# Hyena branch of a two-layer encoder: half-length transforms by even and odd samples, short convolution read from PSUM, and the branch's steps set between projection units

## Chip, cores and metric

The kernel runs on one core of one Trainium2 chip. The metric is the device time of one execution of the whole program, two encoder layers, in microseconds (us). The names of the engines in the profile are PE (TensorE, matrix products), PEld (its weight loads), DVE (VectorE), ACT (ScalarE), POOL (GpSimd) and SP (SyncE, which issues the weight loads from memory).

## What is computed

Two layers over 512 positions of width 1024: a gated feed-forward block, a mixer with three branches, cross-attention to a memory of 256 positions, and a second feed-forward block. The change touches the middle branch of the mixer, the bidirectional Hyena branch of 256 channels:

```python
uc = short_conv(p, conv_w, conv_b)      # three taps over time, per channel
v, x1, x0 = jnp.split(uc, 3, axis=-1)
h = hyena_filters(...)                  # three sine layers of width 64, then w4, times exp(-t * |decay|)
z = x1 * v
# bidir_long_conv: filter = [h_fwd, 0, reversed h_bwd], length 2L
y = irfft(rfft(z, 2L) * rfft(filter), 2L)[:L] + skip * z
return x0 * y
```

The other two branches are a neighbourhood attention ("A") and a dilated attention ("C"), six heads each. All three read the same normed input through one projection.

## The kernel before

**Units.** All large products run as units. A unit is a 128 x 1024 slice of weights: SP loads it into one of two `raw` tiles, ScalarE rounds it to a high half (`high`, L256), VectorE subtracts to get the low half (`low`, L261), and PE multiplies high and low halves of weights and input in 48 instructions of 256 columns (`unit`, L322 to L326). Four units of halves can be ready ahead (`RING`). The result lies in a PSUM bank until an engine has read it out and counted up the semaphore `evac`.

**The mixer's part.** Six Hyena units come first, U_HY = 66 to 71, called Hyena units 0 to 5 here. The first four of them go through `first_units` (L376 to L378) in two halves, since the normed input arrives in halves; 4 and 5 follow as ordinary units. ScalarE copies each result with its neighbours' borders into `p` (L822), VectorE makes the short convolution from it with one instruction of scale and bias and two that add a neighbour (L1101, L1105). Then come 18 units for values, queries and keys of the two attentions, U_VA = 72 to 89, called V0 to V17 here. VectorE copies each out, and V0 to V5 (the values) are then turned by PE in `turn_values`. After V15 attention begins.

**The order of the work** is written out by hand: each engine has a list, and the engines wait for each other at semaphores only. In the list of PE all Hyena steps stand between Hyena unit 4 and V0. They are: three small products for the sine layers (L546, L552), each of which waits for the sine of the one before (L830), which waits for five VectorE steps that reduce the argument (L1117 to L1125); the taps (L556); eight transposes of z (L563); the transforms of the filter (L574) and of z (L583), each 2 parts x 4 blocks of frequency x 4 blocks of time with 256 columns; the product of the spectra on VectorE (L1151 to L1159); the way back (L592), 16 products of 512 columns; and the sums of squares for the norm (L597). Every F32 product shows as two records in the trace. The transforms are products with tables of cosine and sine, `fwd` and `inv`, 2 MB each, which GpSimd's queue loads in every layer.

**GpSimd** also loads the bias strips of attention A (48 small transfers, L1300) once the Hyena branch has left its buffers, and then makes 18 subtractions (L1306) of them before attention may start; the buffers of the Hyena branch and of attention lie in the same memory (`place`), so their order is held by semaphores (`wait_apart`).

Of the kernel before, what the change touches and what calls it, by code (L numbers as in the profile page):

```python
# [36 lines left out]
STRIP = 7 * P  # L37

# [27 lines left out]
def build(nc, x, mem, par, grow, w_first, w_second, w_proj, rpb, t5, fw1, fw23, fw4, fvec, decay,  # L66
          k_emb, k_fwd, k_inv, k_time, k_namask, k_hot, k_lnn, k_eye, out):
    with ExitStack() as ctx:
# [34 lines left out]
        def place(parts):  # L103
# [11 lines left out]
        hH, hL = hid["hH"], hid["hL"]  # L115
        hy = place([
            ("p", [P, 6, T + 2], F32), ("uc", [P, 6, T], F32), ("fwd", [P, 2, 4, T], F32),
            ("inv", [P, 2, 4, T], F32), ("filt", [P, 2, 4, 256], F32), ("taps", [P, 4, 512], F32),
            ("even", [P, 4, 256], F32), ("zt", [P, 4, 256], F32), ("emb", [P, T], F32),
            ("w1", [P, FW], F32), ("w2", [P, FW], F32), ("w3", [P, FW], F32), ("w4", [P, 512], F32),  # L120
            ("fv", [P, 8], F32), ("tneg", [P, 4], F32)])
        at = place([
            ("qA", [P, 3, T], F32), ("kA", [P, 3, T], F32), ("vt", [P, 3, T], F32),
            ("VA", [P, 7, 384], F32), ("biasA", [P, 3, NA_H, 256], F32), ("qC", [P, 3, T], F32),
            ("kC", [P, 3, T], F32), ("VC", [P, 4, 384], F32), ("strip", [P, C_H, STRIP], F32)])


        ac = place([
            ("over_qA", [P, 3, T], F32), ("over_kA", [P, 3, T], F32), ("kCh", [P, 3, T], F32R),
            ("over_VA", [P, 7, 384], F32), ("qCh", [P, 3, T], F32R), ("over_biases", [P, 2, NA_H, 256], F32),  # L130
            ("qCl", [P, 3, T], F32R), ("kCl", [P, 3, T], F32R)])
# [8 lines left out]
        rstrip = strip[:].rearrange("p h n -> p (h n)")[:, 0:NA_H * 384].rearrange(  # L140
            "p (h r c) -> p h r c", h=NA_H, r=WR)
        amask = strip[:].rearrange("p h n -> p (h n)")[:, NA_H * 384:NA_H * 384 + 768].rearrange(
            "p (y n) -> p y n", y=3)
# [36 lines left out]
        pad_zero = sem("pad_zero")  # L180
# [12 lines left out]
        filt_ready = sem("filt_ready")  # L193
        zt_mm = sem("zt_mm")
        zt_ready = sem("zt_ready")
        z_mm = sem("z_mm")
        prod = sem("prod")
        y_mm = sem("y_mm")
# [118 lines left out]
        def _(e):  # L317
# [221 lines left out]
            for L in range(LAYERS):  # L539
# [4 lines left out]
                first_units(u0, 4 * L + 1)  # L544
                e.wait_ge(hy_small, L * 112 + 112)
                e.matmul(bank[4][0:FW, :], hy["w1"][0:EMB, :], hy["emb"][0:EMB, :], start=True,  # L546
                         stop=True).then_inc(f_mm, 1)
                for j in (4, 5):
                    e.wait_ge(evac, E0 + j - 3)
                    unit(u0 + j, u_of, ul_of, j % 4)  # L550
                    e.wait_ge(f_sin, L * 3 + j - 3)
                    e.matmul(bank[4][0:FW, :], hy[f"w{j - 2}"][0:FW, :], tmp[3][0:FW, :], start=True,  # L552
                             stop=True).then_inc(f_mm, 1)
                e.wait_ge(f_sin, L * 3 + 3)
                for m in range(4):
                    e.matmul(bank[4 + m][:], tmp[3][0:FW, m * P:m * P + P], hy["w4"][0:FW, :],  # L556
                             start=True, stop=True).then_inc(taps_mm, 1)
                for half in range(2):
                    e.wait_ge(z_ready, L * 2 + 2)
                    e.wait_ge(taps_ready, L * 7 + half + 1)  # L560
                    for tt in (2 * half, 2 * half + 1):
                        for c in range(HYT):
                            mm = e.transpose(bank[4 + half][:, (tt % 2 * 2 + c) * P:(tt % 2 * 2 + c) * P + P],  # L563
                                             hy["uc"][:, c, tt * P:tt * P + P], eye[:])
                    mm.then_inc(zt_mm, 1)
                e.wait_ge(taps_ready, L * 7 + 7)
                e.wait_ge(hy_loaded, L * 48 + 48)
                e.wait_ge(zt_ready, L * 2 + 2)
                for part in range(2):
                    for half in range(2):  # L570
                        for kt in (2 * half, 2 * half + 1):
                            for m in range(4):
                                rhs = hy["even"][:, m, :] if part == 0 else hy["taps"][:, m, 256:512]
                                mm = e.matmul(bank[4 + 2 * part + half][:, kt % 2 * 256:kt % 2 * 256 + 256],  # L574
                                              hy["fwd"][:, part, m, kt * P:kt * P + P], rhs,
                                              start=m == 0, stop=m == 3)
                        mm.then_inc(filt_mm, 1)
                e.wait_ge(filt_ready, L * 4 + 4)
                for part in range(2):
                    for half in range(2):  # L580
                        for kt in (2 * half, 2 * half + 1):
                            for m in range(4):
# [888 lines left out]
```

## Time and profile before

| | us |
|---|---|
| median of three runs | 2685.17 (2684.04 to 2689.0) |
| the profiled execution, its own time | 2689.14 |
| its span in the trace | 2687.3 |
| PE busy | 2585.8 (96%) |
| VectorE busy | 1027.3 (38%) |
| ScalarE busy | 923.3 (34%) |
| GpSimd busy | 112.9 (4%) |
| mean granted clock of TensorE | 0.98 |

The busy time of an engine is the time in which at least one of its instructions runs. Products overlap in PE's pipeline, so the time that one more product costs is the distance between starts, and not the duration printed with one. The granted clock is a share of 2.4 GHz; 0.5 is the lower level, 1.2 GHz. "Idle before" names the engine and line whose end released the waiting one.

### The profile page before, as it was taken

To read this page: it belongs to the slowest core of one execution; us is meant where nothing else is said; L and a number is where in the kernel's file an instruction comes from. 1 tells how busy PE (TensorE), PEld (TensorE's weight loads), DVE (VectorE), ACT (ScalarE), POOL (GpSimd) and SP (SyncE) were. 2 spreads that over 40 slices of the span, in tenths; PEclk is the share of its full clock that TensorE was granted. 3 is DMA by queue.
4 is the path that set the end of the run, shared out by engine and by line. 5 is a ranking of instruction groups with operands and counts; after the bars stand their busy time and mean duration, and the time that the engine had idled before them with its cause. 6 is when DMAs were issued, how large, how long until landed. Compare 5 with 4: busy or idle time off the path is not lost.

```text
span 2687.3 us, 47605 instructions
## 1 busy us (share of the span) xinstructions
PE 2585.8 (96%) x20484; PEld 2470.9 (92%) x20484; DVE 1027.3 (38%) x1351; ACT 923.3 (34%) x1509; POOL 112.9 (4%) x186
## 2 busy tenths in 40 slices
PE   7999997899999899999999999978999999999998
PEld 7999996698799799999999999966978998999998
DVE  3333236234445453332253332443443643533322
ACT  4333233024533343332253331331254433533322
POOL 0000000140000000000000000103200000000000
PEclk9999997999999999999999999979999999999999
DMA  4322324041024122333232322321300341233222
GB/s 147 94 93 94 99 75 156 22 138 48 1 94 139 52 96 94 94 95 98 87 111 94 94 94 95 117 95 48 136 25 25 102 142 40 95 94 94 94 95 79
DMA packets 66247, 240.62 MB, mean 90 GB/s; under 512 B 8882, under 2 KB 10632, under 8 KB 65088
## 3 DMA queue, kind: packets, MB, share of 16 engines
q1 hardware_dynamic: 57600, 209.74, 24.0%
q0 software_dynamic: 8368, 28.83, 3.3%
q8 instruction: 107, 1.75, 0.3%
q14 instruction: 28, 0.23, 0.0%
q10 hardware_dynamic: 144, 0.07, 0.0%
HBM read 236.48 MB, written 2.12 MB: 89 GB/s over the span
## 4 chain that ended last, share of the span: by engine, by line
PE 88%; DVE 6%; DMA 3%; ACT 2%; issue 1%; POOL 0%; DVEq 0%; ACTq 0%; POOLq 0%
PE bank L322 23%; PE bank L326 23%; PE bank L324 23%; PE bank L515 3%; DMA raw<-in_w_proj 2%; PE bank L490 2%; PE bank L376 2%; PE bank L378 2%; PE bank L377 2%; DVE wl L261 2%; PE bank L574 1%; PE bank L592 1%; PE bank L457 1%; PE bank L583 1%; PE bank L464 1%
## 5 line engine op out<-in xcount | busy, mean ns | idle before, releaser
L261 DVE TENSOR_TENSOR wl<-raw,wh 128x1024 fp32r<-128x1024 f32 x392 | 486.4, 1241 | 482.0 <-ACT wh L256 480.7
L322 PE MATMUL bank<-uH,wh 128*128 128x256 f32 x3328 | 664.4, 281 | 0.0
L326 PE MATMUL bank<-uH,wl 128*128 128x256 f32 x3328 | 661.1, 280 | 0.0
L324 PE MATMUL bank<-uL,wh 128*128 128x256 f32 x3328 | 660.9, 280 | 0.0
L256 ACT ACTIVATE wh<-raw 128x1024 fp32r<-128x1024 f32 x392 | 413.3, 1054 | 706.8 <-PE bank L326 586.1
L322 PEld LDWEIGHTS bank<-uH,wh 128*128 128x128 f32 x3328 | 507.5, 189 | 7.2 <-issue 7.1
L324 PEld LDWEIGHTS bank<-uL,wh 128*128 128x128 f32 x3328 | 507.2, 188 | 0.0
L326 PEld LDWEIGHTS bank<-uH,wl 128*128 128x128 f32 x3328 | 507.0, 188 | 0.0
L973 DVE TENSOR_TENSOR tmp<-bank,tmp 128x512 f32<-128x512 f32 x88 | 60.8, 691 | 629.5 <-PE bank L326 596.8
L322 PE MATMUL bank<-wh,hH 128*128 128x256 f32 x1408 | 281.6, 281 | 0.0
L326 PE MATMUL bank<-wh,hL 128*128 128x256 f32 x1408 | 281.1, 281 | 0.0
L324 PE MATMUL bank<-wl,hH 128*128 128x256 f32 x1408 | 281.1, 281 | 0.0
L326 PEld LDWEIGHTS bank<-wh,hL 128*128 128x128 f32 x1408 | 215.9, 188 | 0.0
L324 PEld LDWEIGHTS bank<-wl,hH 128*128 128x128 f32 x1408 | 215.9, 188 | 0.0
L322 PEld LDWEIGHTS bank<-wh,hH 128*128 128x128 f32 x1408 | 215.7, 188 | 0.0
L734 ACT ACTIVATE hH<-tmp 128x512 f32 x88 | 55.9, 636 | 404.1 <-DVE tmp L973 404.1
L376 PE MATMUL bank<-uH,wh 128*128 128x256 f32 x512 | 146.5, 286 | 9.9 <-DVE uL L940 4.9
L377 PE MATMUL bank<-uL,wh 128*128 128x256 f32 x512 | 144.1, 281 | 0.0
L378 PE MATMUL bank<-uH,wl 128*128 128x256 f32 x512 | 143.9, 281 | 0.0
L731 ACT ACTIVATE tmp<-bank 128x512 f32<-128x512 f32 x88 | 52.5, 597 | 204.9 <-PE bank L326 190.5
L322 PE MATMUL bank<-wh,uH 128*128 128x256 f32 x512 | 105.7, 289 | 6.9 <-DVE uL L1050 3.9
L376 PEld LDWEIGHTS bank<-uH,wh 128*128 128x128 f32 x512 | 97.3, 190 | 11.7 <-DVE wl L261 6.3
(198 smaller groups left out, 2959.0 us busy)
## 6 DMA issues: line engine op xcount, KB each, us to landing
raw<-in_w_first SPq DMA_DIRECT2D x176, 512.0 KB, 3.6
raw<-in_w_proj SPq DMA_DIRECT2D x128, 512.0 KB, 3.5
raw<-in_w_second SPq DMA_DIRECT2D x88, 512.0 KB, 3.5
strip<-bias_of_distance POOLq DMA_DIRECT2D x2, 2688.0 KB, 13.3
g_pre<-in_grow POOLq DMA_DIRECT2D x8, 512.0 KB, 7.2
g_post<-in_grow POOLq DMA_DIRECT2D x8, 512.0 KB, 4.9
fwd<-in_k_fwd POOLq DMA_DIRECT2D x4, 1024.0 KB, 7.0
inv<-in_k_inv POOLq DMA_DIRECT2D x2, 2048.0 KB, 9.4
```

The source lines that it names most:

```text
L256: e.activation(wh[u % RING][:], raw[u % RAWS][:], ACT.Copy).then_inc(high_ready, 1)
L261: e.tensor_tensor(wl[u % RING][:], raw[u % RAWS][:], wh[u % RING][:].bitcast(F32), ALU.subtract).then_inc(split_ready, 1)
L322: e.matmul(b[:, c], still_h, hi[:, c], start=first and c.start == 0, stop=False)
L324: e.matmul(b[:, c], still_h, lo[:, c], start=False, stop=False)
L326: mm = e.matmul(b[:, c], still_l, hi[:, c], start=False, stop=last and c.stop == n)
L376: e.matmul(bank[j][:, n], wh[u % RING][:, w], uH[:, k, n], start=half + k == 0, stop=False)
L377: e.matmul(bank[j][:, n], wh[u % RING][:, w], uL[:, k, n], start=False, stop=False)
L378: mm = e.matmul(bank[j][:, n], wl[u % RING][:, w], uH[:, k, n], start=False, stop=half == 1 and k == DT - 1)
L490: mm = e.transpose(bank[2 + t % 2][:, c * P:c * P + P], tmp[t % 4][:, c * P:c * P + P], eye[:])
L515: mm = e.matmul(O[:, col:col + w], tmp[4 + t % 2][:, c * P:c * P + P], v, start=c == 0, stop=c == chunks - 1)
L734: e.activation(hH[:, bass.ds((2 * it + q) * T, T)], tmp[2 + q][:], ACT.Copy).then_inc(hidh_ready, 1)
L973: e.tensor_tensor(tmp[2 + q][:], bank[2 * q + 1][:], tmp[q][:], ALU.mult).then_inc(h_ready, 1)
```

## The change

**Transforms.** The frequencies run in pairs: the table now holds the lower half of them only (256), and the samples are sorted by parity (`by_parity`). The spectrum of the even samples and that of the odd samples are made apart, each with half the samples and half the frequencies, and their sum and difference give the two halves of the spectrum (`butterflies`). The way back does the same in reverse: four sums and differences on VectorE, then an even and an odd half of y with 256 columns each. The tables are half as large, and z is taken with stride 2 when it is transposed.

**Short convolution.** ScalarE reads a unit's bank with the middle tap as scale and the bias added and writes `uc` (`middle`); VectorE adds the two neighbours with the bank itself as input (`neighbours`). `p` and its borders are gone, and VectorE's second step counts up `evac`.

**Order.** The small products of the sine layers stand behind the first and third Hyena unit and behind unit 4; z is transposed between Hyena units 4 and 5. The spectrum of z stands before V0, and the rest between the V units: taps behind V0, spectrum of the filter behind V1, the way back behind V4, the sums behind V6, with VectorE's steps in its own list at the same places. Since these steps hold banks 4 to 7, `turn_values` uses banks 2 and 3, and V0 to V5 alternate between banks 0 and 1.

**GpSimd.** `inv` is loaded ahead of a wait that it stood behind; the bias strips wait for the transforms of z, the taps and the windows instead of for the finished branch, and their subtractions for the way back.

The diff, cut to its core:

```diff
-            def first_units(u0, b):
+            def first_units(u0, b, between=lambda j: None):
...
                             mm.then_inc(unit_done, 1)
+                            between(j)
...
+                def spectrum(part, parity, moving):
+                    for kt in range(2):
+                        for m in range(2):
+                            mm = e.matmul(bank[4 + 2 * part + parity][:, kt * 256:kt * 256 + 256],
+                                          hy["fwd"][:, part, parity, m, kt * P:kt * P + P], moving[:, 2 * parity + m, :],
+                                          start=m == 0, stop=m == 1)
+                    return mm
+
+                first_units(u0, 4 * L + 1, lambda j: filter_layer(j // 2) if j in (0, 2) else None)
+                e.wait_ge(evac, E0 + 1)
+                unit(u0 + 4, u_of, ul_of, 0)
+                filter_layer(2)
+                e.wait_ge(z_ready, L * 2 + 2)
...
+                e.wait_ge(evac, E0 + 2)
+                unit(u0 + 5, u_of, ul_of, 1)
+                e.wait_ge(hy_loaded, L * 48 + 48)
+                e.wait_ge(zt_ready, L * 2 + 2)
+                e.wait_ge(f_arg, L * 3 + 3)
                 for part in range(2):
...
+                    for parity in range(2):
+                        mm = spectrum(part, parity, hy["zt"])
+                    mm.then_inc(z_mm, 1)
...
+                        for parity in range(2):
+                            for part in range(2):
+                                for kt in range(2):
+                                    cut = slice(kt * 256 + c * P, kt * 256 + c * P + P)
+                                    mm = e.matmul(bank[4 + c][:, parity * 256:parity * 256 + 256],
+                                                  yc[:, 2 * part + parity, cut], hy["inv"][:, part, parity, kt, :],
+                                                  start=part + kt == 0, stop=part + kt == 2)
...
+                hyena = {0: filter_taps, 1: filter_spectrum, 4: back_to_time, 6: hyena_sums}
...
                 for j in range(18):
-                    e.wait_ge(evac, E0 + 6 + j - 3)
-                    unit(L * UNITS + U_VA + j, u_of, ul_of, (6 + j) % 4)
+                    e.wait_ge(evac, E0 + 6 + j - (1 if j < 8 else 3))
+                    if j == 8:
+                        e.wait_ge(vt_out, L * 9 + 9)
+                    unit(L * UNITS + U_VA + j, u_of, ul_of, j % 2 if j < 6 else (6 + j) % 4)
+                    if j in hyena:
+                        hyena[j]()
...
+                    e.activation(hy["uc"][:, UC[j], :], bank[j % 4][:], ACT.Identity,
+                                 scale=pr[:, CW0 + 6 + j:CW0 + 6 + j + 1],
+                                 bias=pr[:, CB0 + j:CB0 + j + 1]).then_inc(conv_mid, 1)
                     high(e, u + RING)
...
+                middle(0)
+                argument(0)
+                middle(1)
+                sine(0)
+                middle(2)
+                argument(1)
+                middle(3)
+                sine(1)
+                middle(4)
+                argument(2)
...
+                    e.wait_ge(conv_mid, L * 6 + j + 1)
+                    e.scalar_tensor_tensor(c[:, 1:T], b[:, 0:T - 1], before, c[:, 1:T], ALU.mult,
+                                           ALU.add).then_inc(conv, 1)
+                    e.wait_ge(conv, L * 6 + j + 1)
+                    e.scalar_tensor_tensor(c[:, 0:T - 1], b[:, 1:T], after, c[:, 0:T - 1], ALU.mult,
+                                           ALU.add).then_inc(evac, 1)
...
+                        if part == 0:
+                            e.tensor_tensor(to[:, 1, :], even, odd, ALU.subtract).then_inc(ready, 1)
+                        else:
+                            e.tensor_tensor(to[:, 3, :], odd, even, ALU.subtract).then_inc(ready, 1)
...
+                for j in range(4):
+                    neighbours(j)
+                    low(e, u0 + j)
+                    if j in (0, 2):
+                        reduced(j // 2)
...
+                butterflies(hy["zf"], zf_even, zf_ready)
+                hyena = {0: tap_values, 1: real_product, 2: imaginary_product, 4: gated, 6: hyena_norm}
...
                     low(e, L * UNITS + U_VA + j + RING)
+                    if j in hyena:
+                        hyena[j]()
...
+                e.dma_start(hy["inv"][:], k_inv).then_inc(inv_loaded, 16)
                 wait_apart(e, u_ready, (4 * L + 1) * NT + NT)
                 e.dma_start(tmp[0][:], decay[L:L + 1].to_broadcast([P, 512])).then_inc(hy_loaded, 16)
-                e.dma_start(hy["inv"][:], k_inv).then_inc(inv_loaded, 16)
                 gains(L, 4 * L + 2)
 
-                wait_apart(e, hyout, L * 6 + 4)
+                wait_apart(e, z_mm, L * 2 + 2)
+                wait_apart(e, taps_mm, L * 4 + 4)
+                wait_apart(e, window, L * 4 + 4)
...
+                wait_apart(e, y_mm, L * 2 + 2)
                 for y, c0 in enumerate((16, 8, 0)):
```

How the lists move, at three places. First PE's list before, layer 0, from Hyena unit 4 to V0 (the rows `bank<-uH,wh` are the first product of a unit; `tmp,w` are the sine layers, `w,tmp` the taps, `eye,uc` the transposes of z, the last row with `tmp,ones` the sums):

```order
L322 MATMUL bank<-uH,wh 128x256 [waits split_ready,evac]
...
L552 MATMUL bank<-tmp,w 64x512 [waits f_sin]
L556 MATMUL bank<-w,tmp 128x512 [waits f_sin]
...
L563 MATMUL bank<-eye,uc 128x128 [waits taps_ready,z_ready]
...
L574 MATMUL bank<-even,fwd 128x256 [waits zt_ready,hy_loaded,taps_ready]
...
L574 MATMUL bank<-taps,fwd 128x256 x16
L583 MATMUL bank<-zt,fwd 128x256 [waits filt_ready]
L583 MATMUL bank<-zt,fwd 128x256 x31
L592 MATMUL bank<-inv,taps 128x512 [waits inv_loaded,prod]
L592 MATMUL bank<-inv,taps 128x512 x15
L597 MATMUL bank<-tmp,ones 128x512 [waits hysq] x2
L322 MATMUL bank<-uH,wh 128x256 [waits split_ready,evac]
```

All of it lies in a row, from the second sine layer to the sums, without a unit in between. Now PE's list after the change, from Hyena unit 4 to the spectrum of the filter behind V1:

```order
L328 MATMUL bank<-uH,wh 128x256 [waits split_ready,evac]
...
L560 MATMUL bank<-tmp,w 64x512 [waits f_sin]
L580 MATMUL bank<-eye,uc 128x128 [waits z_ready]
...
L328 MATMUL bank<-uH,wh 128x256 [waits split_ready,evac]
...
L566 MATMUL bank<-zt,fwd 128x256 [waits f_arg,zt_ready,hy_loaded]
L566 MATMUL bank<-zt,fwd 128x256 x15
L328 MATMUL bank<-uH,wh 128x256 [waits split_ready,evac]
...
L598 MATMUL bank<-w,tmp 128x512 [waits zf_ready,f_sin]
...
L328 MATMUL bank<-uH,wh 128x256 [waits split_ready,evac]
...
L566 MATMUL bank<-even,fwd 128x256 [waits taps_ready]
L566 MATMUL bank<-even,fwd 128x256 x7
L566 MATMUL bank<-taps,fwd 128x256 x8
```

Between each two Hyena steps stands a unit, the product of z with `fwd` has moved ahead of the taps, and it and that of the filter have half their instructions. Last VectorE's list after the change, from the copy of V1 (`vt<-bank`) on, where `wl` is a weight's low half, `zf` and `filt` are the spectra, and `Y` their product:

```order
L1296 COPY vt<-bank 128x8x64 [waits unit_done]
L267 TENSOR_TENSOR wl<-raw,wh 128x1024 [waits high_ready]
L1198 TENSOR_TENSOR filt<-filt,bank 128x512 [waits filt_even]
L1200 TENSOR_TENSOR filt<-bank,filt 128x512 [waits filt_even]
L1204 TENSOR_TENSOR filt<-filt,bank 128x512 [waits filt_ready] x2
L1232 TENSOR_TENSOR Y<-zf,filt 128x1024 [waits filt_ready,zf_ready]
L1233 TENSOR_TENSOR even<-zf,filt 128x1024
L1235 TENSOR_TENSOR Y<-Y,even 128x1024 [waits prod]
L1296 COPY vt<-bank 128x8x64 [waits unit_done]
L267 TENSOR_TENSOR wl<-raw,wh 128x1024 [waits high_ready]
L1239 TENSOR_TENSOR Y<-zf,filt 128x1024
L1241 TENSOR_TENSOR even<-zf,filt 128x1024 [waits prod]
```

Behind the copy of V1 the filter's butterflies and the real product now stand, and the copy of V2 comes behind them; before, no Hyena step stood behind any of these copies.

## Rows read from the trace of the kernel before

**Rows 1.** The page: span, busy time of the engines, chain that ended last.
```profile
span 2687.3 us, 47605 instructions
...
PE 2585.8 (96%) x20484; PEld 2470.9 (92%) x20484; DVE 1027.3 (38%) x1351; ACT 923.3 (34%) x1509; POOL 112.9 (4%) x186
...
PE 88%; DVE 6%; DMA 3%; ACT 2%; issue 1%; POOL 0%; DVEq 0%; ACTq 0%; POOLq 0%
```

**Rows 2.** Windows of layers 0 and 1; the columns are in the first line.
```profile
core 0: us, PE busy (x) PEld busy (x) DVE busy (x) ACT busy (x) POOL busy (x), PEclk, DMA share, GB/s
426.30:525.70 99.40, 75.28 (x284) 51.73 (x284) 36.26 (x54) 20.27 (x28) 1.17 (x3) 0.81 0.09 33
525.70:625.00 99.30, 99.30 (x849) 98.84 (x848) 36.64 (x36) 22.95 (x29) 43.40 (x66) 1.00 0.40 129
1755.30:1854.60 99.30, 75.04 (x293) 51.70 (x292) 36.34 (x55) 21.02 (x30) 2.08 (x4) 0.83 0.11 36
1854.60:1954.00 99.40, 99.40 (x847) 98.47 (x846) 41.61 (x37) 22.64 (x29) 41.53 (x65) 1.00 0.39 127
```

**Rows 3.** PE's waits, 426.3 to 525.7: line, releaser, total us, times, longest.
```profile
PE bank L592 <- DVE taps L1159: 8.0, 1, 8.0
PE bank L556 <- ACT tmp L830: 6.3, 1, 6.3
PE bank L552 <- ACT tmp L830: 6.0, 1, 6.0
...
PE bank L583 <- ACT filt L847: 0.7, 1, 0.7
```

**Rows 4.** PE's timeline, 426 to 530: start, us, line, tiles, count, idle before.
```profile
439.12 1.96 PE L552 MATMUL bank<-tmp,w 64*64 64x512 f32 x2 [6.00 <-ACT tmp L830]
...
448.77 1.07 PE L552 MATMUL bank<-tmp,w 64*64 64x512 f32 x2
...
456.15 7.19 PE L556 MATMUL bank<-w,tmp 64*128 64x512 f32 x8 [6.31 <-ACT tmp L830]
463.27 1.97 PE L563 MATMUL bank<-eye,uc 128*128 128x128 f32 x8
...
484.53 14.08 PE L583 MATMUL bank<-zt,fwd 128*128 128x256 f32 x64 [0.69 <-ACT filt L847]
506.56 15.79 PE L592 MATMUL bank<-inv,taps 128*128 128x512 f32 x32 [7.95 <-DVE taps L1159]
522.19 1.02 PE L597 MATMUL bank<-tmp,ones 128*128 128x512 f32 x2
```

**Rows 5.** VectorE's timeline, 395 to 585.
```profile
419.18 1.54 DVE L1105 SCALAR_TENSOR_TENSOR uc<-p,pr,uc 128x512 f32<-128x512 f32 x2
420.64 1.22 DVE L261 TENSOR_TENSOR wl<-raw,wh 128x1024 fp32r<-128x1024 f32 x1
...
435.65 0.41 DVE L1117 TENSOR_SCALAR tmp<-tmp 64x512 f32<-64x512 f32 x1
...
458.82 0.69 DVE L1130 TENSOR_TENSOR taps<-bank,tmp 128x512 f32<-128x512 f32 x1 [3.39 <-ACT tmp L839]
...
531.42 1.22 DVE L1180 COPY vt<-bank 128x512 f32<-128x512 f32 x1 [2.81 <-PE bank L326]
...
557.35 2.02 DVE L261 TENSOR_TENSOR wl<-raw,wh 128x1024 fp32r<-128x1024 f32 x1 [0.46 <-ACT wh L256]
```

**Rows 6.** ScalarE's timeline, 395 to 585.
```profile
428.92 1.06 ACT L256 ACTIVATE wh<-raw 128x1024 fp32r<-128x1024 f32 x1 [4.75 <-DMA raw<-in_w_proj]
...
431.31 0.76 ACT L827 ACTIVATE tmp<-bank,fv 64x512 f32<-64x512 f32 x1
432.09 1.28 ACT L830 ACT_TABLE_LOAD   x1
438.44 0.63 ACT L830 ACTIVATE tmp<-tmp 64x512 f32<-64x512 f32 x1 [5.06 <-DVE tmp L1125]
```

**Rows 7.** GpSimd's timeline, 395 to 760.
```profile
525.07 25.02 POOL L1300 DMA_DIRECT2D strip<-in_rpb  x48
551.90 18.14 POOL L1306 TENSOR_TENSOR biasA<-strip 128x256 f32<-128x256 f32 x18 [1.80 <-DMA strip<-in_rpb]
```

More of the change, by code:

```diff
@@ L197, in build @@
         prod = sem("prod")
+        y_ready = sem("y_ready")
         y_mm = sem("y_mm")
@@ L543, in _ @@
                 u0 = L * UNITS + U_HY
[L544 to L553, printed above, removed]
@@ L578, in _ @@
[L578 to L582, printed above, removed]
-                                mm = e.matmul(bank[6 - 2 * part + half][:, kt % 2 * 256:kt % 2 * 256 + 256],
-                                              hy["fwd"][:, part, m, kt * P:kt * P + P], hy["zt"][:, m, :],
-                                              start=m == 0, stop=m == 3)
-                        mm.then_inc(z_mm, 1)
@@ new lines, in filter_spectrum, with back_to_time @@
+                def filter_spectrum():
+                    e.wait_ge(taps_ready, L * 7 + 7)
+                    for part in range(2):
+                        for parity in range(2):
+                            mm = spectrum(part, parity, hy["even"] if part == 0 else hy["taps"][:, :, 256:512])
+                        mm.then_inc(filt_mm, 1)
+                def back_to_time():
+                    e.wait_ge(y_ready, L * 4 + 4)
+                    e.wait_ge(filt_ready, L * 4 + 4)
+                    e.wait_ge(inv_loaded, L * 16 + 16)
+                    yc = hy["taps"]
+                    for c in range(HYT):
+                        for parity in range(2):
+                            for part in range(2):
+                                for kt in range(2):
[3 more added lines that the diff above has]
+                                                  start=part + kt == 0, stop=part + kt == 2)
+                        mm.then_inc(y_mm, 1)
@@ new lines, in sine, with windows @@
+                def sine(n):
+                    e.wait_ge(f_red, L * 15 + 5 * n + 5)
+                    e.activation(tmp[3][0:FW, :], tmp[1][0:FW, :], ACT.Sin).then_inc(f_sin, 1)
+                def windows(ms):
+                    for m in ms:
+                        if m >= 2:
+                            e.wait_ge(taps_ready, L * 7 + m - 1)
+                        e.activation(tmp[1 + m % 2][:], tmp[0][:], ACT.Exp,
+                                     scale=hy["tneg"][:, m:m + 1]).then_inc(window, 1)
@@ L831, in _, with even_half @@
+                sine(2)
+                middle(5)
+                def even_half(to, product, copied):
+                    for part in range(2):
+                        e.wait_ge(product, L * 2 + part + 1)
+                        e.activation(to[:, 2 * part, :], bank[4 + 2 * part][:], ACT.Copy).then_inc(copied, 1)
+                even_half(hy["zf"], z_mm, zf_even)
                 load_log_exp()
```

325 lines of the change are left out of this document (166 added, 159 removed).

## The prediction, made before the changed kernel ran

> **What bounds the kernel now.** I read the page first. PE is busy 96% of the span and PE work makes up 88% of the chain that ended last [rows 1], so what counts is time in which PE does less than it could. I cut the trace at the places where the Hyena branch begins and ends. Each layer has a stretch of 99.4 and 99.3 us between the end of the fourth Hyena unit and the first value unit, and one of 99.3 and 99.4 us that holds the 18 value, query and key units [rows 2]. The second kind is full: PE busy throughout, clock 1.00, 849 records of products. The first kind has 284, a clock of 0.81 and 0.83, and VectorE and ScalarE busy only 36 and 20 us. The two layers agree to 0.1 us, so I work out layer 0 and double it. In that stretch PE waits six times, 8.0, 6.3 and 6.0 us down to 0.7, 24 us in all [rows 3]: the longest three are for the product of the spectra and for two sines. The third view is PE's own timeline there [rows 4]. The reader is to see two things in it: how long each matrix step takes, and that steps behind a wait run at the lower clock (1.2 GHz; eight records of 512 columns in 7.19 us, but two in 1.02 us once the clock is up).
>
> **Prices.** A record is one of the two passes that an F32 product leaves. At the upper clock (2.4 GHz) a 256-column record steps every 0.22 us (64 in 14.08) and a 512-column one every 0.43 (1.02 for two, less the 0.59 in which the last runs out, its shortest record) [rows 4]. A unit has 48 records; at 99.3 us for 849 [rows 2] it takes 5.6.
>
> **The change on PE, layer 0.** Before, the stretch is 99.4 us. After, the same jobs are:
> - three filter layers, two records each, 1.07 at the upper clock [rows 4] and 1.0 to the next start: 3.0
> - Hyena units 4 and 5: 11.2
> - eight transposes of z: 1.97 us at the lower clock [rows 4], so 1.0 at the upper
> - spectrum of z: 16 products instead of 32, so 32 records of 256 columns: 7.05
> - filter taps, eight records of 512 columns: 3.45 (7.19 before)
> - spectrum of the filter, 32 records: 7.05 (64 records before)
> - back to time: 16 products of 256 columns instead of 16 of 512, so 32 records: 7.05 (15.79 before)
> - sums of squares, four records of 512 columns: 1.7
>
> That is 41.5 us if PE never waits, 57.9 less than 99.4. The 18 units behind keep their 99.3 us; only their place changes. Of the 57.9 about 21 come from halving at the upper clock (twice 32 x 0.22, and 32 x 0.21), 24 from the waits, 13 from the clock and from restarts.
>
> **The waits that stay.** I walked the four queues, in the order that the excerpts above show, with the durations of [rows 5, 6], from 417.9, the end of the first Hyena unit (426.3 [rows 2] less three half units of 2.8). (1) First sine: eviction 0.6, weight half 1.05, argument 0.76 bring ScalarE to 420.3; VectorE has two neighbour steps of 0.76 and a weight half of 1.2 and is free at 421.4; the reduction takes 2.8 to 424.2, the sine 0.6 to about 425.1. PE arrives at 424.3 (filter layer and two half units of 2.8): it waits 0.8. The table load of 1.3 fits beside the reduction. (2) z: VectorE does neighbours, weight half and reduction for units 1 to 3 and the two products (1.3 together) at about 436.9; PE arrives at 435.6: 1.3. If the raw load that took 7 us before (it ended at 428.9, where ScalarE had been idle for 4.75 us [rows 6]) is as late again, z comes 1.4 later; it should come earlier, as 1.25 MB instead of 3.25 MB is queued by GpSimd at that point (the constants are half as large and the inverse one goes ahead of the wait). (3) Butterflies of z end near 453.6, PE wants the taps at 456.4: hidden. (4) Taps: behind V0 VectorE has a copy of 1.2, a weight half 1.2, four tap products, the memset and two 1024-wide steps, 8.2 in all; PE covers that with the taps' products (3.45) and V1 (5.6): 9.0, so 0.8 us to spare. The thinnest cover. (5) Butterflies of the filter (4 x 0.69), six 1024-wide products (1.22 each, as the weight half), four 512-wide sums (0.65 each), with two copies and weight halves between: y_ready near 487.5, PE arrives near 491.6. (6) Two banks instead of four: unit Vj waits for the copy of V(j-2). That of V2 starts when the real product is done, 478.9, with V2 itself; that of V3 is done at 488.2, and V5 wants it at 499. Hidden. (7) The squares of y are done near 507, PE asks at 511. The copy out of PSUM in a new order may cost 1.2 where it costs 0.7, as the strided copy does [rows 5]; it has those 4 us.
> Everything else stands beside this: the evictions' scale and bias ride on ScalarE; the tap windows lie behind V0; the 48 bias strips (25.0 us of issue [rows 7]) start near 461 instead of 524, their 18 subtractions near 499, and attention wants them at V15, near 550.
> So 2.1 us of waits, and 0.9 for restarts: 3 a layer. Gain 57.9 - 3 = 55 a layer, **110 in all**. The profiled execution took 2689.1 us around a span of 2687.3; its span would become 2577. The median of the runs is 2685.2, 4 us below that execution; I take the gain from the median: 2575, and put **2576**.
>
> **GpSimd beside VectorE.** A weight half on VectorE took 2.02 us instead of 1.22 while GpSimd ran the 18 subtractions [rows 5, 7]. Those now start behind the way back, beside V5 to V8, where VectorE has a copy and a weight half per unit of 5.6 us (2 to 3 us of work) and the end of the branch; a delay of 0.8 on each weight half is covered, and the sum stands. The Trainium skill (SBUF — State Buffer, section Who interferes with whom) says that a VectorE instruction with both inputs in SBUF and a GpSimd one that reads SBUF contend for the shared read port; the 2.02 agrees. By it the six spectrum products would be slowed too, were GpSimd's subtractions beside them; the list keeps them behind.
> **The clock.** After the 6.0 us of waiting for the first sine, two records of 512 columns took 1.96 instead of 1.07, and the unit behind it 7.6 instead of 5.6 (441.1 to 448.8) [rows 4]: a fall costs 2.9 us. Behind a wait of 0.7 us [rows 3] the 64 records of z ran at 0.22 each [rows 4], the upper clock, so I take no fall for waits of 1 us. If each of the two waits did cost one, the sum would be 110 less 2 x 2 x 2.9, and the time 2588. The Trainium skill (TensorE: Matmul & The Clock Gate, What's actually happening) has the low clock as the default that activity lifts; it names no price for a single short wait, and these rows agree with it.
>
> **Rivals.**
> *A, waits come back.* Covers (4), (5) and (6) hang on VectorE, which carries some 45 us of work between 444 and 502. For: 0.8 us of cover at (4); the contended 2.02. Against: the subtractions come behind step (5). If VectorE's instructions there take a third longer, that is 15 us, of which the covers take 5; 10 a layer are lost: 2596.
> *B, clock falls at the two short waits:* 2588, as above, where what speaks against it stands too. For it: one of the two is twice as long as the 0.7 us.
> *C, lock step, slower than before.* All VectorE's work from Hyena unit 2 to V7 (about 60 us by the prices above) and 8 us of ScalarE's are outside PE's. Then the stretch holds 41.5 + 68 = 109.5 instead of 99.4, the time is 2705. It decides from 58 of the 68 us uncovered; two banks would have to give no overlap at all. Against: 36 us of VectorE's work lay beside full PE work in the second stretch of each layer already [rows 2], and PE always has the next unit allowed.
> *D, the records do not halve in time:* narrower inverse products step at half of 0.43 only if the weight load hides. If each stepped at 0.43, back to time would keep 13.8: 6.7 a layer, 2589. Against: 256-column records with a new stationary tile each already step at 0.22.
>
> **How the numbers follow.** Forecast 0.70, A 0.17, B 0.06, D 0.04, C 0.02, anything else 0.01. No waits at all would give 110 + 6 = 116 and 2569, with 3 us for the spread of runs: low end 2566. The high end takes in B, D and the larger part of A: 2598. A measurement can tell about 0.2% (5 us) from no change; all cases but C lie far beyond it: faster 0.97, same 0.01, slower 0.02.
>
> **What would show it.** Between the fourth Hyena unit and the first attention score of each layer the stretch of 199 us should be 143 or 144, PE busy almost throughout and the clock 1.00 in both halves; three lines of 32 records at 0.22 us each. PE's list of waits there should have only the first sine and z, near 1 us each; a wait for the taps is A at (4), one for a VectorE copy A at (6), one for y_ready A at (5). Two pieces at 0.43 per 256 columns would be B or D. The forecast is wrong if those waits together pass 8 us a layer, or if the 18 units themselves stretch.

## The result: 2585 us instead of 2685, 2570 to 2581 when the clock stays up

| | us |
|---|---|
| changed kernel, median of 4 executions (lowest, highest) | 2585.5 (2570.2, 2628.8) |
| kernel before, median of 4 beside it | 2684.6 (2680.3, 2689.0) |
| ratio, 95% interval | 0.9614 (0.9587 to 0.9642) |
| profiled execution of the changed kernel, its span | 2570.2, 2568.3 |
| profiled execution before, its span | 2689.1, 2687.3 |

The changed kernel has executions that take 20 or 50 us longer at a lower TensorE clock; the ratio leaves out those 50 us longer, and all readings of traces are of an execution at 2570 unless the text says otherwise. 2576 was forecast. Span against span the gain is 119.0 us where 110 was forecast, but these two traces are the longest of the four executions before and the shortest of all sixteen that the changed kernel had in this study. Its eight executions near 2575 average 2575.3 us, 109 below the 2684.6 beside them.

The page answers to [rows 1]: PE's busy time is 69.6 us shorter, and its share of the chain went from 88% to 90%.
```profile
span 2568.3 us, 47339 instructions
...
PE 2516.2 (98%) x20356; PEld 2431.4 (95%) x20356; DVE 1034.0 (40%) x1347; ACT 924.4 (36%) x1509; POOL 115.3 (4%) x186
...
PE 90%; DVE 4%; DMA 3%; ACT 2%; issue 1%; SPq 0%; DVEq 0%; ACTq 0%
```
The windows answer to [rows 2]. The 199 us of each layer (a stretch at clock 0.81 and one at 1.00) are now one stretch that PE fills at 1.00, and VectorE is busy for 54% of it (the second line is the inner part of layer 1's).
```profile
426.30:570.00 143.70, 143.70 (x1094) 135.42 (x1093) 76.96 (x91) 41.44 (x56) 45.19 (x68) 1.00 0.34 108
1700.00:1850.00 150.00, 149.78 (x1126) 139.95 (x1126) 81.11 (x94) 42.21 (x61) 45.32 (x68) 1.00 0.32 106
```
PE's waits from 395 to 600, the same columns as [rows 3]. Of 8.0, 6.3 and 6.0 us one of 1.0 is left; the other two lines belong to the unit ahead of the branch and to attention, and stand in both kernels. Layer 1 has the same three.
```profile
PE bank L560 <- ACT tmp L873: 1.0, 1, 1.0
PE bank L382 <- DVE wl L267: 0.7, 1, 0.7
PE bank L522 <- ACT tmp L797: 0.2, 1, 0.2
```
PE's timeline there, to be read against [rows 4]. The three transforms take 7.07, 3.61 + 3.62 and 7.07 us where 14.08, 14.1 (by 64 x 0.22) and 15.79 stood; the eight records of the taps run at the upper clock, 3.70 instead of 7.19; only the first sine is waited for.
```profile
417.94 1.07 PE L560 MATMUL bank<-emb,w 33*64 33x512 f32 x2
...
425.77 1.07 PE L560 MATMUL bank<-tmp,w 64*64 64x512 f32 x2 [0.96 <-ACT tmp L873]
...
435.44 1.07 PE L560 MATMUL bank<-tmp,w 64*64 64x512 f32 x2
436.44 1.23 PE L580 MATMUL bank<-eye,uc 128*128 128x128 f32 x8
...
443.11 7.07 PE L566 MATMUL bank<-zt,fwd 128*128 128x256 f32 x32
...
455.71 3.70 PE L598 MATMUL bank<-w,tmp 64*128 64x512 f32 x8
...
465.11 3.61 PE L566 MATMUL bank<-even,fwd 128*128 128x256 f32 x16
468.56 3.62 PE L566 MATMUL bank<-taps,fwd 128*128 128x256 f32 x16
...
491.14 7.07 PE L620 MATMUL bank<-inv,taps 128*128 128x256 f32 x32
...
510.14 1.88 PE L629 MATMUL bank<-tmp,ones 128*128 128x512 f32 x4
```
VectorE's timeline at the covers that the forecast walked [rows 5]: z, the last step of the taps, the last sum ahead of the way back, and a weight half beside GpSimd's subtractions.
```profile
434.58 1.29 DVE L1278 TENSOR_TENSOR uc<-uc 128x512 f32<-128x512 f32 x2
...
462.45 1.22 DVE L1219 TENSOR_TENSOR taps<-taps 128x1024 f32<-128x1024 f32 x1
...
485.74 1.29 DVE L1249 TENSOR_TENSOR taps<-Y 128x512 f32<-128x512 f32 x2
...
505.45 1.51 DVE L267 TENSOR_TENSOR wl<-raw,wh 128x1024 fp32r<-128x1024 f32 x1 [0.46 <-ACT wh L262]
```
The taps end at 463.7 and PE wants them at 465.1; the last sum ends at 487.0 and PE wants it at 491.1.

**The gain by place.** Two of PE's waits stand in both kernels, and PE's work is the same in front of the first and behind the second, up to the next layer: one of 0.70 us for a weight's low half, ahead of the branch, and one of 0.56 us in part A of attention, behind it. The distance between them is what branch and units take. Before, in layers 0 and 1:
```profile
408.37 0.39 PE L376 MATMUL bank<-uH,wh 128*128 128x256 f32 x1 [0.70 <-DVE wl L261]
669.86 0.66 PE L515 MATMUL bank<-VA,tmp 128*128 128x64 f32 x4 [0.56 <-ACT tmp L761]
1737.48 0.39 PE L376 MATMUL bank<-uH,wh 128*128 128x256 f32 x1 [0.70 <-DVE wl L261]
1997.81 0.66 PE L515 MATMUL bank<-VA,tmp 128*128 128x64 f32 x4 [0.55 <-ACT tmp L761]
```
and after:
```profile
408.46 0.39 PE L382 MATMUL bank<-uH,wh 128*128 128x256 f32 x1 [0.70 <-DVE wl L267]
613.63 0.66 PE L522 MATMUL bank<-VA,tmp 128*128 128x64 f32 x4 [0.56 <-ACT tmp L797]
1677.29 0.39 PE L382 MATMUL bank<-uH,wh 128*128 128x256 f32 x1 [0.70 <-DVE wl L267]
1882.46 0.66 PE L522 MATMUL bank<-VA,tmp 128*128 128x64 f32 x4 [0.56 <-ACT tmp L797]
```
That is 261.5 and 260.3 us before and 205.2 in both layers after: 56.3 and 55.2 us won, 111.5 in all. Two more traces of the changed kernel (numbers 1 and 7) give 205.1 and 205.2 again, so this distance is the yardstick below.

The other 7.5 us of the 119.0 lie outside the branches: 4.0 between the wait of attention in layer 0 and the branch of layer 1, and 3.7 behind the attention of layer 1, less 0.1 at the start. Part of it is cross-attention, where PE waits for the normed values (3.6 and 4.9 us before, 2.2 and 2.3 after) and where in the trace before three windows of 20 us stand at clock 0.91 and in this one none. But the changed kernel's own trace of number 7 has such falls too, and it is 2.3 us longer than this one in the first piece and 1.4 in the second. The same 20 us around cross-attention's start in layer 0, before, after, and in number 7:
```profile
880.00:900.00 20.00, 16.29 (x89) 13.92 (x89) 9.08 (x14) 7.65 (x19) 0.00 (x0) 0.91 0.33 110
820.00:840.00 20.00, 16.90 (x110) 15.04 (x109) 9.44 (x14) 7.90 (x18) 0.00 (x0) 1.00 0.39 133
820.00:840.00 20.00, 17.20 (x102) 14.82 (x101) 8.97 (x13) 7.89 (x17) 0.00 (x0) 0.91 0.39 133
```
So 111.5 us are the change's, and of the rest of this pair's 119 about half is a difference between executions of one kernel.

### The profile page after: what moved, and what is told of

Same layout as the page of the kernel before. It is cut to its first block, busy times and chain, and to the rows that moved or that the text cites. A ratio compares the mean times of both kernels' runs of the same rounds, so it can differ in the third digit from the quotient of the medians.

```text
span 2568.3 us, 47339 instructions
## 1 busy us (share of the span) xinstructions
PE 2516.2 (98%) x20356; PEld 2431.4 (95%) x20356; DVE 1034.0 (40%) x1347; ACT 924.4 (36%) x1509; POOL 115.3 (4%) x186
## 4 chain that ended last, share of the span: by engine, by line
PE 90%; DVE 4%; DMA 3%; ACT 2%; issue 1%; SPq 0%; DVEq 0%; ACTq 0%
PE bank L328 24%; PE bank L330 24%; PE bank L332 24%; PE bank L522 3%; DMA raw<-in_w_proj 2%; PE bank L382 2%; PE bank L497 2%; PE bank L383 2%; PE bank L384 2%; DVE wl L267 1%; PE bank L566 1%; PE bank L471 1%; ACT wh L262 1%; PE bank L369 1%; PE bank L464 1%
```

## Experiments

Theory H1 is the forecast's: the gain is half order (steps between units) and half less PE work, and PE stays fed. Its rivals are A to D; of these C and D fell with the trace above. What was open is how the gain divides, how thin the covers are, and why executions of one kernel lie 50 us apart. On the last the expectations name three theories: K (what they lose is TensorE's clock in one stage, the rest being the same), F (the sparse products at the turn from part A to part C of attention decide) and H (a fall of the clock in the branch, or any shift of the work, keeps it from happening there).

**1. The changed kernel again, five rounds.** No edit.


> The changed kernel once more, in five rounds. Its profiled execution took 2570, with one wait of 1.0 us in the Hyena part of a layer, but its other runs 2575, 2596 and 2629 with mean granted clocks of 0.995, 0.985 and 0.973. Theory K (the clock falls somewhere, in some executions, and nothing else differs): time and clock go together on one line, about 24 us for 0.01 of clock, and the runs spread again over some 2570 to 2630. Rival (the first runs were disturbed by chance): the runs agree within 10 us of 2572 and the clock is 0.995 to 0.997 in all.


Six executions: 2574.8, 2578.5, 2596.8, 2599.4, 2622.8, 2623.7; eleven of before beside them 2679.8 to 2689.6. Time and clock go together as theory K says: 0.995 at 2574.8, 0.983 at 2599.4, 0.973 at 2623.7, some 22 us for 0.01. The profiled one was one of the long ones, and its windows show the place. Layer 1, part A of attention, then part C, then the piece behind it:
```profile
1860.00:1885.00 25.00, 24.44 (x149) 17.94 (x148) 17.55 (x59) 19.27 (x65) 0.00 (x0) 1.00 0.00 1
1885.00:1990.00 105.00, 105.00 (x384) 84.01 (x383) 25.87 (x80) 34.83 (x92) 0.00 (x0) 0.50 0.00 1
1990.00:2000.00 10.00, 10.00 (x54) 9.13 (x54) 1.66 (x6) 3.96 (x11) 0.00 (x0) 0.61 0.01 2
```
The same 105 us in the execution of 2570:
```profile
1885.00:1990.00 105.00, 100.70 (x727) 88.49 (x727) 36.63 (x97) 46.41 (x117) 0.56 (x1) 0.97 0.09 31
```
At clock 0.50 (1.2 GHz) PE does 384 records where it does 727. From the wait of 0.56 us to the first transposes behind part C this execution takes 119.8 us and the other 68.7, so this piece holds 51 of the 53.5 us between their spans. At the turn from A to C the two timelines show the same records and the same wait of 0.56 us, until the clock falls at 1885:
```profile
1883.97 0.66 PE L522 MATMUL bank<-VA,tmp 128*128 128x64 f32 x4 [0.56 <-ACT tmp L797]
1884.56 0.70 PE L471 MATMUL bank<-kA,qA 64*128 64x256 f32 x2
1885.19 0.68 PE L497 MATMUL bank<-eye,tmp 128*128 128x128 f32 x2
```
In the Hyena branch the two have the same waits, and between the two waits 205.1 and 205.2 us. So the 50 us are lost in attention, by a fall of the clock that this kernel runs into and the kernel before, in 4 + 11 executions, did not.

**2. The same steps, in a row ahead of the first value unit** (new arithmetic, old place).
```diff
+                for step in hyena.values():
+                    step()
                 for j in range(18):
...
-                    if j in hyena:
-                        hyena[j]()
```
(the same in VectorE's list; ScalarE's steps stand ahead of its units too)


> Halved transforms and convolution from PSUM as in the change, but the steps behind the spectrum of z (taps, filter, way back, sums) stand in a row ahead of V0 again, on PE, VectorE and ScalarE. Theory (order gives back the waits and the clock): PE waits about 2.6 us for z's butterflies, 3.6 for the taps, 12.6 for the product of the spectra and 2.1 for the squares, 21 a layer, and some 5 a layer for the lower clock behind the long one: 2572 + 52 = 2624. Rival (halving alone carries the gain, the waits would have been covered by the pipeline anyway): 2575.


2633.7 (2630.3 to 2635.8, 4 executions), ratio 0.981 (0.9795 to 0.9826); 2624 was expected. Between the two waits of the yardstick layer 0 takes 234.2 us and layer 1 238.5, 29.0 and 33.3 more than the changed kernel. The waits are back, PE from 395 to 600:
```profile
PE bank L620 <- DVE taps L1244: 12.4, 1, 12.4
PE bank L566 <- DVE taps L1214: 3.6, 1, 3.6
PE bank L598 <- DVE zf L1199: 2.7, 1, 2.7
PE bank L629 <- ACT tmp L916: 1.6, 1, 1.6
```
and the clock from 426 to 500 is 0.79. These waits are 20.3 us, where 21 was expected; the lower clock behind them costs 8.4 and not 5 (taps 7.16 us instead of 3.70, first half of the filter's spectrum 6.53 instead of 3.61, way back 9.05 instead of 7.07). Layer 1 has one wait more, 3.6 us for the copy of a value unit. It stands behind VectorE's last two steps of the branch, which ran there while GpSimd made its 18 subtractions (1792.4 to 1808.2) and took 12.29 us; in layer 0, beside the same subtractions, they took 2.62:
```profile
1797.07 12.29 DVE L1262 SCALAR_TENSOR_TENSOR yb<-yb,pr,side 128x512 f32<-128x512 f32 x2 [3.27 <-ACT side L921]
```
So with the new arithmetic the order of the steps behind the spectrum of z is worth 58 us by the executions, and 62 in this trace, somewhat more than half of the gain.

**3. Each transform's products done twice** (the old amount of PE work, in the new order).
```diff
-                        for m in range(2):
+                        for m in (0, 1, 0, 1):
...
-                        for parity in range(2):
+                        for parity in (0, 0, 1, 1):
```


> The changed kernel with every product of the two transforms and of the way back made twice (the same result), so as many records of 256 columns as the old transforms had records (the way back with half its old columns each). Order as in the change. Theory (PE is full there, each record costs its 0.22 us): 96 more records a layer, 21.1 us, 42 in both: 2614. Rival (some of the records hide in waits of PE that remain): under 2600. Rival (the records of the way back step slower than 0.22): over 2620.


2619.0, 2620.5, 2669.3, 2669.4; 2614 was expected. Between the two waits it takes 225.8 and 225.9 us, 20.7 more in each layer. The spectrum of z on PE's timeline:
```profile
444.10 13.97 PE L566 MATMUL bank<-zt,fwd 128*128 128x256 f32 x64
```
No wait came or went in the branch. The halving is worth 41 us in all; the lower pair is 44 above 2575.3, and the rest of the difference lies outside the branches. Two of four executions lie 50 us higher again, so more work in the branch, without a wait, did not take the spread away.

**4. The short convolution from SBUF, as before, in the new order.** ScalarE copies the bank into a padded buffer; VectorE does three steps instead of two.
```diff
-                    e.activation(hy["uc"][:, UC[j], :], bank[j % 4][:], ACT.Identity,
-                                 scale=pr[:, CW0 + 6 + j:CW0 + 6 + j + 1],
-                                 bias=pr[:, CB0 + j:CB0 + j + 1]).then_inc(conv_mid, 1)
...
+                    e.activation(hyp[:, j, 1:T + 1], bank[j % 4][:], ACT.Copy).then_inc(conv_mid, 1)
...
+                    e.tensor_scalar(c, hyp[:, j, 0:T], cw[0], pr[:, CB0 + j:CB0 + j + 1], ALU.mult,
+                                    ALU.add).then_inc(conv, 1)
```
(this is the first of its three steps; the two others add the middle and the next sample, from the same buffer)


> The changed kernel with the short convolution as before: ScalarE copies the unit to p with borders, VectorE makes three instructions from it. VectorE has 0.55 us more per Hyena unit, ScalarE 0.18 less. Theory (only the thin places count): the first sine comes 0.4 us later and z about 2 us later, so 1 to 2 us a layer, 2574 to 2577. Rival (VectorE is what the whole part hangs on): 6 x 0.55 us a layer and more, over 2580. In its lines VectorE's instructions from PSUM and from SBUF can be compared, 0.75 each in the trace of the change.


2580.6 (2575.6 to 2582.3, 4 executions), where 2574 to 2577 was expected. Between the two waits it takes 208.3 and 206.8 us, 3.1 and 1.6 more than the changed kernel. VectorE's extra 0.55 us per unit makes z late, and PE waits for it in both layers. In layer 0 the products behind the wait ran at the lower clock (1.79 where 1.23 stood), in layer 1, behind the same wait, they did not:
```profile
437.57 1.79 PE L582 MATMUL bank<-eye,uc 128*128 128x128 f32 x8 [1.84 <-DVE uc L1283]
1711.87 1.23 PE L582 MATMUL bank<-eye,uc 128*128 128x128 f32 x8 [1.84 <-DVE uc L1283]
```
A neighbour step takes 0.75 us from SBUF,
```profile
418.80 0.75 DVE L1178 SCALAR_TENSOR_TENSOR uc<-p,pr,uc 128x512 f32<-128x512 f32 x1
```
and 0.75 from PSUM:
```profile
418.93 0.75 DVE L1171 SCALAR_TENSOR_TENSOR uc<-bank,pr,uc 128x511 f32<-128x511 f32 x1 [4.07 <-ACT uc L857]
```
So it is the step saved that counts. Order 58 to 62, halving 41 and short convolution 5 make 104 to 108 of the 111.5. Each is the price of taking one part out of the changed kernel, and they need not add up to the whole: with half the products there is less to cover the spectra's product, and in number 2 it is waited for 12.4 us where the kernel before waited 8.0. The Trainium skill (VectorE: DVE Perf Modes, Rules for kernel authors) offers for elementwise work on a matmul's output either to take the slower mode or to copy to SBUF first where many operations follow; for these two-input F32 steps the rows show nothing to be won by the copy.

**5. The taps 6 us late** (six more VectorE sums of 128x1024, 1.2 us each, ahead of the taps' last two steps).
```diff
+                    for n in range(6):
+                        e.tensor_tensor(hy["even"][:], taps[:, :, 0:256], taps[:, :, 256:512],
+                                        ALU.add).then_inc(late, 1)
+                        e.wait_ge(late, L * 6 + n + 1)
```


> The changed kernel with six extra 1024-wide VectorE instructions (each 1.2 us, the same result as the one they repeat) ahead of the last two steps of the taps. Two questions. Cover: in the trace of the change the last tap step ends 1.4 us before PE has finished V1, so 7.4 us more should make PE wait 6.0 us a layer for the taps. With the fall of the clock behind a wait of 6 us (2.9 to 5 us) this is 9 to 11 us a layer, a fastest run near 2572 + 20 = 2592. Rival for the cover (VectorE's delay runs on into the copies and the product of the spectra and is paid more than once): over 2600. Spread: theory H (a fall and rise of the clock in the Hyena part, which the kernel before has in each layer, keeps the clock from staying down in the attention behind it, as in the kernel before and in e2): the runs agree within 8 us. Rival P (whether the clock falls at the turn from attention A to C is chance and independent of what ran 130 us earlier): the runs spread by 20 and 50 us again, in about half of them.


2588.5, 2591.2, 2589.2, 2589.2, 2589.0. Two rows of PE's timeline:
```profile
470.57 5.64 PE L567 MATMUL bank<-even,fwd 128*128 128x256 f32 x16 [6.01 <-DVE taps L1224]
476.05 3.62 PE L567 MATMUL bank<-taps,fwd 128*128 128x256 f32 x16
```
7.5 us more work met 1.4 us of cover and left a wait of 6.0, and the fall of the clock behind it cost 2.0 (5.64 against 3.61). Between the two waits it takes 213.4 and 213.3 us, 8.3 and 8.1 more, which is the sum. Behind the wait everything else had room. This prices cover (4), and shows what rival A would have looked like. All five executions lie within 3 us of each other; 2592 was expected.

**6. Two idle products of 512 columns in each of seven attention steps around the turn from A to C.**
```diff
+                    if part == "mixer" and 20 <= s < 27:
+                        w = wh[U_WO % RING]
+                        if s == 20:
+                            e.wait_ge(o_split, L * 32 + 6)
+                        for _ in range(2):
+                            e.matmul(bank[7][:], w[:, 0:P], w[:, 0:T], start=True, stop=True)
```


> The changed kernel with two products of 512 columns, whose result nobody reads, in each of the seven attention steps around the turn from attention A to C, where the clock fell to 0.50 for about 115 us in the profiled execution of e1. Theory F (the clock falls there because PE does too little in these steps): no run is 20 or 50 us above the fastest, the clock is 0.992 or more in all. Price: if PE bounds these steps 14 x 0.22 = 3 us a layer, so 2575 to 2578. Rival (the fall has its cause elsewhere, or the other falls lie elsewhere): the spread stays.


2577.2, 2578.5, 2579.1, 2582.0, 2583.1: none 20 or 50 us above. The products come on top of three such idle products in each of the attention steps 2 to 6, which both kernels have (`KEEP_BUSY`).

**7. The changed kernel a third time, five rounds beside number 6.** No edit.


> The changed kernel itself on the same chip, as the yardstick of the two: by what it did so far, four of ten executions near 2575, four near 2597 and three near 2625, clock 0.995, 0.984 and 0.973. Where a profile with 0.984 is caught: theory (one attention stage, in part) the clock stands at 0.50 for about 50 us in one of the two attention stages; rival: somewhere in the feed-forward part.


2572.6, 2573.8, 2576.0, 2581.0, 2626.7, 2627.9. The profiled one, 2573.8, was a short one. Over all 16 executions of the changed kernel eight took 2570 to 2581, three 2596 to 2599 and five 2623 to 2629; their mean is 2595.3.

**8. One idle product a step instead of two.** The edit of number 6 with `range(1)`.


> The changed kernel with ONE idle product of 512 columns, instead of two, in each of the seven attention steps around the turn from part A to part C. Theory F (the sparse products around that turn decide whether the clock falls there, and filling them keeps it up): if one product is enough, all five executions within 10 us of each other and none 20 or 50 us above; each added product stands partly in PE's path, so the time is 2 to 3 us above the fast executions of the changed kernel, 2573 to 2580. If one is too little, one or two of five near 2600 or 2625. Rival H (any shift of the work removes the fall by chance): says the same here, so the run beside this one decides.


2577.1, 2577.2, 2577.5, 2578.4, 2580.0; ratio to before 0.9597 (0.9585 to 0.961). Their mean is 2578.0: 17 us below the changed kernel's mean of sixteen, 3 above that of its eight short executions (2575.3; number 6 is 5 above). It has the lowest mean of all versions, on a chip on which the changed kernel itself was not run (before has 2684.4 there and 2684.9 beside numbers 5 to 7); numbers 4 and 6, at 2579.8 and 2580.0, are hardly behind.

**9. The two idle products ten steps earlier**, in the middle of part A.
```diff
+                    if part == "mixer" and 10 <= s < 17:
```


> The changed kernel with the same two idle products of 512 columns in seven attention steps, but ten steps earlier (steps 10 to 16, in the middle of part A), so that the turn from part A to part C is as sparse as in the changed kernel. Theory F (what counts is the filling at the turn): the spread stays; of five executions about three lie 20 or 50 us above the lowest, and the lowest is at 2573 to 2582. Rival H (any added work, or a fall or fill anywhere before, removes it): five executions within 10 us of each other at 2575 to 2583.


2578.8, 2580.2, 2581.3, 2584.1, 2584.4, 2627.2. One of six had the full 50, so idle products as such don't end it. Theory F expected about three of five, theory H none: neither came. With the products at the turn it was none of ten (numbers 6 and 8), where the changed kernel had eight of sixteen. By chance alone, an estimate from these counts, none of ten would come about once in 120 times; but if only the executions that are 50 us above count (five of sixteen) once in 15, and none of ten can't be told from one of six.

## Why the prediction was right

- **The PE sum held to the row.** 41.5 us of work in place of the stretch of 99.4: third filter layer 1.07, transposes 1.23 (1.0 forecast), three lines of 7.05 came as 7.07, 7.23 and 7.07, taps 3.70 (3.45), squares 1.88 (1.7). The stretch of 199 us is 142.5, where 143 or 144 was forecast, with PE busy throughout. Doubling the halved work (number 3) cost 20.7 us a layer where "about 21 come from halving" was put; "24 from the waits, 13 from the clock and from restarts" are 37 us, of which putting the steps back in a row brought 29.0 and 33.3. The old first stretch also had the sines' waits without any unit between; number 2 keeps the filter's layers between the Hyena units, so 37 was not tested whole.
- **Wait (1), first sine:** 0.96 against 0.8. (The walk's own terms put PE there at 424.5, not 424.3; it came at 424.8, and the sine 0.7 later than walked.)
- **Wait (2), z:** 1.3 forecast, none came. The walk had z ready at 436.9 and PE there at 435.6; they were 435.9 and 436.4. VectorE was 1 us sooner than walked, and PE 0.8 later. Half a microsecond of cover is little: number 4 lost it by 0.55 us of work per unit.
- **Cover (4), "the thinnest":** 1.4 us to spare where 0.8 was put. Number 5 shows what lies behind it.
- **Covers (3), (5), (6), (7)** held. For (5) the forecast had 487.5 against 491.6; it was 487.0 against 491.1.
- **Restarts,** put at 0.9 a layer: the gain was 56.3 and 55.2 against 55, so in layer 0 waits, restarts and all that was put too low came to 1.6 and not 3. "Gain 57.9 - 3 = 55 a layer, 110 in all" missed the two branches by 1.5 us. The 7.5 us that this pair of traces has outside them are no term of the sum, and number 7's trace shows that half of them come and go between executions of the changed kernel.
- **Rivals.** A did not come, but what was said against it rests on layer 0 alone. "The two layers agree to 0.1 us", and so the contended weight half was priced at 2.02; in layer 1 of the same trace one took 7.18 us, and after the change one took 5.27 there:
```profile
1891.32 7.18 DVE L261 TENSOR_TENSOR wl<-raw,wh 128x1024 fp32r<-128x1024 f32 x1 [0.47 <-ACT wh L256]
```
```profile
1774.28 5.27 DVE L267 TENSOR_TENSOR wl<-raw,wh 128x1024 fp32r<-128x1024 f32 x1 [0.46 <-ACT wh L262]
```
In layer 0 they took 1.5 where 2.0 was put. Both times PE did not wait for it. The forecast had shown that for "a delay of 0.8 on each weight half" and not for one of 4 to 6: here it was lucky. By the Trainium skill (SBUF — State Buffer, Who interferes with whom) the two engines contend for a shared read port, and 1.51 and 5.27 against 1.22 agree. B: behind the 0.96 us of wait two records took 1.07, the upper clock. C: VectorE's 77 us lay beside PE's work. D: records of the way back step at 0.22.
- **The range** (2566 to 2598) holds the median, and 2576 lies on the mean of the short executions, 2575.3. It would not have held six of the sixteen executions, and the median of number 1 (2598.1) only just falls outside it: that the median of four came to 2585 is luck of the draw. The forecast looked for the clock in the branch that changed, and the risk was in attention.

## What to carry to other kernels

When the bounding engine's waits come from a serial side branch, cut the branch into steps and place each behind enough independent work of that engine; then walk every queue with durations from the trace, since covers of half a microsecond to one and a half decide. Price waits at what stands behind them too: here a wait of 6 us cost 8. Read the prices in every layer, not in one: the same instruction took 2.0 us in one and 7.2 in the other. And take several executions before a difference of 1% is believed: the same code had medians of 2585, 2598 and 2579 here.

## What the runs showed that was not expected

**A lower clock that stays while PE is busy.** In number 1 PE's clock fell from 2.4 to 1.2 GHz at the turn from A to C and stayed there for more than 100 us, though the window shows PE busy 105.00 of 105.00 us. In the execution of 2570 part C ran at 1.00 with PE busy for 63.81 of the 65 us from 1885 to 1950, and most of the 4.3 us that it is idle in the 105 lie behind part C, so busy time alone does not tell the two apart. The one fall that a profile caught cost 51 us, 2% of the time. The Trainium skill (TensorE: Matmul & The Clock Gate, What's actually happening) has activity release the lower clock; here over 100 us of a PE that the profile calls busy did not. What lifts the clock again is not shown: it rose near the end of part C, with the clock at 0.61 from 1990 to 2000.

**One VectorE instruction beside GpSimd can take six times its time.** A weight half alone takes 1.22 us. The longest beside GpSimd's 18 subtractions took 2.02 and 7.18 in layers 0 and 1 of the kernel before, 1.5 to 1.6 in layer 0 of the new order (numbers 1 and 3 to 9) and 1.8 to 6.1 in layer 1; the three traces of the changed kernel have 5.3, 1.8 and 1.8 there, so it differs between executions of one kernel. In the changed kernel none of this reached PE. In number 2 it did, by 3.6 us, because the steps of the branch stood right ahead of the value units' copies.

**What the spread hangs on stays open.** Numbers 6 and 8 (idle products at the turn) had none of ten, number 9 (elsewhere) one of six. But numbers 4 and 5, whose attention stage is unchanged and which only lose 2 to 8 us a layer in the branch, had none of nine, number 2 none of four, and the kernel before none in all its executions here. In those traces the clock dips briefly in the branch (in number 5 behind the 6.0 us wait; in number 4 behind 1.84), which none of the changed kernel's traces show. Two readings fit: a fall in the branch keeps the later one from happening, or any small shift changes the odds. Against the first stands that number 4's trace has the dip in layer 0 only (the clock is 1.00 throughout the branch of layer 1), while the one long fall that was caught came in the attention of layer 1. A deliberate dip with everything else in place, over some ten executions, would tell them apart, and was not tried. The executions near 2597 were never caught in a profile; their granted clock (0.983 to 0.985) says that their 20 us too are clock, but not where they lie.
